# A bidirectional RWKV-7 scan on TensorE: the second direction's data move to the other head's partitions, and the fillers get a new order

## The reference, cut to what matters

```python
def step(S, inp):
    r_t, w_t, k_t, v_t, a_t, b_t = inp
    sa = einsum('zdhij,zdhj->zdhi', S, a_t)
    S = S * w_t + sa[..., :, None] * b_t[..., None, :] + v_t[..., :, None] * k_t[..., None, :]
    y = einsum('zdhij,zdhj->zdhi', S, r_t)
    return S, y
```

## Time and profile before

| | us |
|---|---|
| median of 3 runs | 2592.85 (2590.28 to 2593.1) |
| profiled execution: span from first to last instruction | 2592.7 |
| main loop of the scan, t = 0 to 39, in that execution | 593.71 |
| TensorE busy in the span | 2466.9 |
| VectorE, ScalarE, GpSimd busy in the span | 1183.0, 720.9, 806.8 |

### The profile page before, as it was taken

The page is one execution under the profiler, slowest core; times in us unless marked ns, Lnnn a source line. Parts: engine busy times, 40 slices in busy tenths (PEclk is TensorE's granted clock), DMA queues, the critical chain, the costliest instruction groups (busy, mean ns, idle before and its releaser), DMA issues. The chain is left out here.

```text
span 2592.7 us, 63094 instructions
## 1 busy us (share of the span) xinstructions
PE 2466.9 (95%) x27732; PEld 2043.2 (79%) x27732; DVE 1183.0 (46%) x2490; ACT 720.9 (28%) x1804; POOL 806.8 (31%) x623
## 2 busy tenths in 40 slices
PE   7999999999999699999999889999999999999997
PEld 6785568888888588778888767878888888888885
DVE  4105660000233466665766475554444444444446
ACT  5115661011111355645545432211110001110013
POOL 3322212222232233333333264023333224332234
PEclk9999999999999799999999989999999999999999
DMA  6110011111110100000000062211101010111014
GB/s 166 45 33 18 1 50 65 74 73 58 49 41 25 43 4 4 4 4 4 4 4 4 3 252 90 84 54 49 41 34 40 33 48 34 41 41 33 33 65 146
DMA packets 39085, 123.08 MB, mean 47 GB/s; under 512 B 11424, under 2 KB 11424, under 8 KB 37664
## 3 DMA queue, kind: packets, MB, share of 16 engines
q1 hardware_dynamic: 38816, 119.06, 13.5%
HBM read 96.24 MB, written 20.97 MB: 45 GB/s over the span
## 5 line engine op out<-in xcount | busy, mean ns | idle before, releaser
L2122 DVE TENSOR_TENSOR ff_f<-ff_f,ff_ps 128x512 f32<-128x512 f32 x300 | 205.3, 686 | 173.7 <-PE ff_ps L98 173.7
L2039 ACT ACTIVATE ff_rl<-ff_ps 128x512 f32<-128x512 f32 (+1 forms) x96 | 50.6, 527 | 754.9 <-PE ff_ps L98 754.9
L2141 DVE TENSOR_TENSOR ff_sq<-ff_rl 128x512 f32<-128x512 f32 (+1 forms) x96 | 125.5, 1308 | 271.9 <-ACT ff_rl L2039 271.7
L1058 DVE TENSOR_TENSOR sc_q<-sc_ps,sc_cs 128x128 f32<-128x128 f32 x400 | 98.4, 281 | 195.5 <-PE sc_ps L465 193.7
L1908 POOL TENSOR_TENSOR ff_wd0h<-ff_wdr,params 128x1024 fp32r<-128x1024 f32 x16 | 30.3, 1894 | 458.7 <-DMA ff_wdr<-in_w_down 458.7
L815 ACT ACTIVATE sc_xy<-sc_ps 128x256 f32<-128x256 f32 x320 | 116.5, 387 | 173.1 <-PE sc_ps L481 171.0
L481 PE MATMUL sc_ps<-sc_xy,sc_q 64*64 64x64 f32 x3200 | 150.7, 221 | 6.7 <-DVE sc_q L1058 6.0
L98 PE MATMUL ff_ps<-hh,ff_wu0h 128*128 128x512 f32 (+1 forms) x384 | 136.6, 356 | 4.4 <-issue 4.4
L98 PE MATMUL ff_ps<-hl,ff_wu0h 128*128 128x512 f32 (+1 forms) x384 | 136.3, 355 | 0.0
L98 PE MATMUL ff_ps<-hh,ff_wu0l 128*128 128x512 f32 (+1 forms) x384 | 136.3, 355 | 0.0
L98 PE MATMUL ff_ps<-hh,ff_wu1h 128*128 128x512 f32 (+1 forms) x384 | 136.0, 354 | 0.0
(11 more groups left out here) (323 smaller groups left out, 7007.2 us busy)
## 6 DMA issues: line engine op xcount, KB each, us to landing
ff_wur<-in_w_up SPq DMA_DIRECT2D x32, 512.0 KB, 3.5
ff_wdr<-in_w_down SPq DMA_DIRECT2D x32, 512.0 KB, 4.3
gwr<-in_w_in SPq DMA_DIRECT2D x31, 512.0 KB, 3.5
gm_dram<-gp_gm SPq DMA_DIRECT2D x8, 1280.0 KB, 4.4
ff_m<-gm_dram SPq DMA_DIRECT2D x16, 640.0 KB, 7.8
fr_x<-in_x SPq DMA_DIRECT2D x10, 512.0 KB, 5.1
ff_xs<-in_x SPq DMA_DIRECT2D x10, 512.0 KB, 4.5
x_dram<-ff_xo SPq DMA_DIRECT2D x10, 512.0 KB, 2.9
```

Source lines behind the costliest of these rows:

```text
L1058: nc.vector.tensor_tensor(Q1[g][:, :, :], q_out[g], joins[:, l, :].rearrange("p (u t) -> p u t", u=2), ALU.mult).then_inc(q_ready, 1)
L2039: nc.scalar.activation(rl[v % 2][:, 0:tn], ps[:, b, 0:tn], ACT.Relu).then_inc(relu, 1)
L2122: nc.vector.tensor_tensor(own, own, ps[:, 4 + v % 4, :], ALU.add).then_inc(added, 1)
L2141: nc.vector.tensor_tensor(sq[v % 2][:, 0:tn], rl[v % 2][:, 0:tn], rl[v % 2][:, 0:tn], ALU.mult).then_inc(squared, 1)
```

## The change

Direction 1's data that lie by token (the gram GM, the tokens TK with v now among them, P, U, the state S) move to the partitions of the other head (`on(rows, u)`), so `gram_and_tokens` (the two old functions in one), `outputs` and the others go straight for u = 0 and across for u = 1. Y changes sides from level to level (`y_side`); the flips and VT are gone, and v is turned each time. Arrays a and r of direction 1 and its edges are copied to the other half by two SBUF-to-SBUF transfers a step into SW (SyncE, semaphores `swapped`). The state is the sum of the new part and the old state, then multiplied by the edge, in two VectorE operations, and `keep` is gone. The gram is masked in one operation of 128x512, and the token copy waits for it. The fillers get another order on all three engines.

```diff
-        AR = [sb(f"sc_ar{n}", [P, 4, 2, BT]) for n in range(2)]
-        edge = [sb(f"sc_edge{n}", [P, GR, 2]) for n in range(2)]
+        AR = [sb(f"sc_ar{n}", [P, 2, ENDS + 4 * BT]) for n in range(2)]
+        SW = [sb(f"sc_sw{n}", [P, 2 * ENDS + 2 * BT]) for n in range(2)]
+        array = lambda par, n: AR[par][:, :, ENDS + n * BT:ENDS + (n + 1) * BT]
+        two = lambda par, rows, u, n, g: AR[par][rows, u, ENDS + n * BT:ENDS + (n + 2) * BT].rearrange(
+            "p (n t) -> p n t", n=2)[:, :, chunk(u, g)]
+        own_edge = lambda par: AR[par][:, 1, 0:ENDS]
+        edges = lambda par: SW[par][:, 0:2 * ENDS].rearrange("p (u g) -> p u g", u=2)
...
-        TK = [sb(f"sc_tk{g}", [P, 2, 2, C]) for g in range(GR)]
+        TK = [sb(f"sc_tk{g}", [P, 2, 3, C]) for g in range(GR)]
...
+        on = lambda rows, side: other[rows.start] if side else rows
...
+        def y_side(l, g, u):
+
+            if l == 0:
+                return u
+            if g % HALF == 0:
+                return 1 if l == LEVELS else 0
+            return l % 2
+
+        def q_cross(l, g, u):
+
+            return u ^ y_side(l, g, u)
+
+        def y_cross(l, g, u):
+
+            return y_side(l, g, u) ^ y_side(l + 1, g, u)
...
+            for q in range(STEPS):
+                sp.wait_ge(arr_ready, q + 1)
+                for rows in heads:
+                    sp.dma_start(SW[q % 2][on(rows, 1), ENDS:], AR[q % 2][rows, 1, 0:ENDS + 2 * BT]
+                                 ).then_inc(swapped[q % 2], 16)
...
+            def gram_and_tokens(q, g):
+                ct, i = divmod(q, NB)
                 n = q * GR + g
                 pe.wait_ge(arr_ready, q + 1)
                 if n:
                     pe.wait_ge(masked, n)
-                x = AR[q % 2]
-                for u in range(2):
-                    for m, lhs in enumerate((2, 3)):
+                    pe.wait_ge(tok_ready, n)
...
+                for m in range(2):
+                    for u in range(2):
                         for rows in heads:
+                            nc.tensor.matmul(gram_out[on(rows, u), u, m * 2 * C:(m + 1) * 2 * C],
+                                             array(q % 2, 2 + m)[rows, u, chunk(u, g)], two(q % 2, rows, u, 0, g),
+                                             start=True, stop=True)
+                for m, unit in enumerate((neg_eye, eye)):
+                    for u in range(2):
+                        for rows in heads:
+                            nc.tensor.matmul(tok_out[on(rows, u), u, m * C:(m + 1) * C],
+                                             array(q % 2, 2 + m)[rows, u, chunk(u, g)], unit[rows, :],
+                                             start=True, stop=True)
                 for u in range(2):
                     for rows in heads:
+                        last = nc.tensor.matmul(tok_out[on(rows, u), u, 2 * C:3 * C],
+                                                sT[rows, ct + 2 * CT, tokens(i, u, g)], eye[rows, :],
+                                                start=True, stop=True)
                 last.then_inc(tok_ps, 1)
...
+            def next_x(q, l, g):
+                for u in range(2):
+                    side = y_side(l, g, u)
+                    for rows in heads:
+                        last = nc.tensor.matmul(x_at(l, g, u)[on(rows, u), :], y_in(l, g, u)[on(rows, side), :],
+                                                Q1[g][on(rows, side), u, :], start=True, stop=True)
+                return last
+
+            def next_y(q, l, g):
+                for u in range(2):
+                    side, to = y_side(l, g, u), y_side(l + 1, g, u)
+                    for rows in heads:
+                        last = nc.tensor.matmul(y_at(l, g, u)[on(rows, to), :], Q1[g][on(rows, side), u, :],
+                                                y_in(l, g, u)[on(rows, side), :], start=True, stop=True)
+                return last
...
+                if l == LEVELS - 1:
+                    last = next_y(q, l, g)
+                elif g % HALF == 0:
+                    next_x(q, l, g)
+                    last = next_y(q, l, g)
+                else:
+                    next_y(q, l, g)
+                    last = next_x(q, l, g)
...
+                        a = SW[q % 2][:, 2 * ENDS:2 * ENDS + BT] if u else AR[q % 2][:, 0, ENDS:ENDS + BT]
...
+                pe.wait_ge(s_ready, n + 1)
...
-                if inner:
-                    solved(qs, sa)
-                if levels:
+                    pe.wait_ge(masked, q * GR + gb + 1)
                     pe.wait_ge(tok_ready, q * GR + gb + 1)
                 side(t, 0)
                 if ahead:
                     lora_products(q + 2)
+                if inner:
+                    solved(qs, sa)
                 if levels:
                     level_q(q, 1, ga)
                     level_q(q, 1, gb)
                 if inner:
                     state_out(qs, sa)
-                    outputs(qs, sa)
                 if levels:
                     level_xy(q, 1, ga)
                     level_xy(q, 1, gb)
+                side(t, 1)
                 if ahead:
                     pe.wait_ge(ta_ready, q + 3)
                 if more:
-                    gram_products(qa, sa)
-                if inner:
-                    state_in(qs, sb_)
+                    gram_and_tokens(qa, sa)
                 if levels:
                     level_q(q, 2, ga)
                     level_q(q, 2, gb)
-                side(t, 1)
-                if more:
-                    by_token(qa, sa)
                 if inner:
-                    solved(qs, sb_)
+                    outputs(qs, sa)
                 if levels:
                     level_xy(q, 2, ga)
                     level_xy(q, 2, gb)
                 if inner:
-                    state_out(qs, sb_)
-                if more:
-                    pe.wait_ge(masked, qa * GR + sa + 1)
-                side(t, 2)
-                if more:
-                    pe.wait_ge(tok_ready, qa * GR + sa + 1)
-                side(t, 5)
+                    state_in(qs, sb_)
                 if levels:
                     level_q(q, 3, ga)
                     level_q(q, 3, gb)
                 if inner:
-                    outputs(qs, sb_)
-                side(t, 3)
-                if more:
-                    gram_products(qa, sb_)
+                    solved(qs, sb_)
                 if levels:
                     level_xy(q, 3, ga)
                     level_xy(q, 3, gb)
+                if more:
+                    pe.wait_ge(masked, qa * GR + sa + 1)
+                    pe.wait_ge(tok_ready, qa * GR + sa + 1)
+                side(t, 2)
+                side(t, 5)
+                if inner:
+                    state_out(qs, sb_)
                 if levels:
                     level_q(q, 4, ga)
                     level_q(q, 4, gb)
+                side(t, 3)
                 side(t, 4)
                 if more:
-                    by_token(qa, sb_)
+                    gram_and_tokens(qa, sb_)
+                if inner:
+                    outputs(qs, sb_)
                 if levels:
                     level_xy(q, 4, ga)
                     level_xy(q, 4, gb)
-                if t + 1 < PAIRS:
-                    flip(qa, sa)
-                    flip(qa, sb_)
...
+                act.wait_ge(masked, n + 1)
+                nc.scalar.activation(TK[g][:, :, :, :].rearrange("p u n t -> p u (n t)"), tok_out,
...
-                if inner:
-                    u_copy(qs, sa)
-                    keep(qs, sa)
                 if ahead:
                     lora_tanh(q + 2, 0)
                     lora_tanh(q + 2, 1)
+                if inner:
+                    u_copy(qs, sa)
                 if squares_y and t % 2:
                     y_square(ct - 1, 1)
                 if levels:
...
                     level_copy(q, 1, gb)
                 if late:
                     decays(q + 1, 0)
-                if inner:
-                    p_copy(qs, sb_)
-                    keep(qs, sb_)
+                if levels:
+                    level_copy(q, 2, ga)
+                    level_copy(q, 2, gb)
                 if more:
                     token_copy(qa, sa)
                 if inner:
-                    u_copy(qs, sb_)
-                if levels:
-                    level_copy(q, 2, ga)
-                    level_copy(q, 2, gb)
+                    p_copy(qs, sb_)
                 if late:
                     decays(q + 1, 1)
+                if inner:
+                    u_copy(qs, sb_)
                 if squares_y and t % 2 == 0:
                     y_square(ct - 1, 0)
+                if levels:
+                    level_copy(q, 3, ga)
+                    level_copy(q, 3, gb)
                 if squares_y and t % 2:
                     y_std(ct - 1, GRAM_BANK)
                 if t % 2 and i == 0 and ct + 1 < CT:
                     k_norm(ct + 1, TOK_BANK)
```

(44 more changed lines are left out.)

254 lines of the change are left out of this document (114 added, 140 removed).

## The result

The changed kernel takes 2610.6 us (median of four runs, 2609.1 to 2615.1), the kernel before 2591.6 on the same chip: a ratio of 1.007, 95% interval 1.0058 to 1.0082, slower by 0.7%. The forecast was 2585.

A forecast was written before the change was run, and what follows sets the result against it. TensorE, busy 95% of the span, was taken as the bound. Half step terms, side work, reciprocals and GpSimd waits summed to 585.5 us for the loop against 593.7, -8.2, giving 2585 us, own range 2570 to 2600.

The forecast's parts named there:

- TensorE's saving: Products on other array quarters, mainly gram, tokens, outputs and flips: 2.05 to 2.6 us less per half step, 82 to 105 over 40.
- The idle time before the second chunk's level_q: At the start of a half step TensorE waits for collect, mask and the chain to the transpose: some 1.4 us idle.
- Odd half steps with LoRA products: 18 of 20 odd half steps: 14.5 us each, slower than before, with 2.24 for u_copy and 0.33 for half.
- Even ones without side products: Six even half steps: 11.95 us each, plus 0.7 for VectorE operations waiting on GpSimd.
- The transfers: Two SBUF transfers per step: hidden, first read a half step after the gram; up to 5 us a step if not covered.
- Rival 3: Gram, tokens and outputs do not run four quarters wide: 1.6 us a half step back on the path, 2650; chance 0.05.
- rival 1: Queues hurt less, half of the 1.4 idle and of 2.24 in nine odd half steps goes: 2547; chance 0.13.
- the sum: All loop terms added: 585.5 us against 593.7, so -8.2 and a kernel of 2585.
- rival 4: New idle stretches bring ten more TensorE stretches at 1.2 GHz: +12 us, 2597; chance 0.12.
- the even half steps with side products: 14 even half steps: 11.95 us plus 2.4 for side products, and 0.2 for GpSimd.
- The 2.24 us of u_copy behind the tanh: Odd half steps: state_out waits for u_copy behind four tanh and starts at 11.97 instead of 9.73; bounds 1.5 and 2.6.
- Rival 2: GpSimd blocks the new state multiply and AI in every even half step, 40 us instead of 7: 2618; chance 0.20.

The follow-up runs named there:

- experiment 8: The changed kernel with each gram product made twice into the same columns: 2637.9 us, ratio 1.0179.
- experiment 3: The changed kernel with three extra unused products between the first products of the first and second chunk of each half step: 2603.5 us, ratio 1.0043.
- experiment 10: VectorE's add, multiply, transpose of the first group and half of the LoRA step put behind level 3's joins: changed kernel 2619.1 us, the improved version 2583.2.
- Experiment 1: The changed kernel with u_copy put back ahead of the tanh, and solved ahead of the side and LoRA products: 2593.0 us, ratio 0.9997.
- experiment 11: State update's decay multiply moved from VectorE to ScalarE as two scaled copies: changed kernel 2608.1 us, the improved version 2572.5.
- the improved version: The changed kernel with u_copy ahead of the tanh, the last collect behind the next group's start, and three extra products in the gap: 2579.8 us, ratio 0.9945.
- experiment 7: The changed kernel with gram and token products issued direction by direction, neighbours two quarters at a time: 2614.3 us, ratio 1.0079.

## Why the prediction was wrong, by its own steps

**Right.** TensorE's saving: 2.05 to 2.6 us a half step forecast, 2.0 less busy time measured (just under the lower bound, with 27 us more of the loop at half clock), and in experiment 8 added work costs most of its price. The idle time before the second chunk's level_q: 1.4 us forecast, 58.7/39 = 1.5 measured. Odd half steps with LoRA products: 14.5 plus reciprocal, by_head and GpSimd (together 0.8 to 0.9) is 15.3 to 15.4, and those at full clock take 15.4. Even ones without side products: 11.95 + 0.7 = 12.65, against 12.58 for t = 2 and 13.35 for t = 6. The transfers never appear as a releaser. Rival 3 is out (a block of 20 products for grams and tokens takes 0.79 us, as reckoned for four quarters), and rival 1 is too: the wait for the transpose is as long as said.

**The step that failed is the sum: it left out rival 4 and took the even half steps with side products and the end of the loop too short.** The loop is 20.7 us longer than the sum (606.2 against 585.5). About 10 of it is half clock, as worked out above; the forecast had this as rival 4 with +12 and a chance of 0.12, on the ground that "the new gaps are followed by denser products". The runs speak against that ground: each half step now opens with a gap of 1.5 us in the mean, and five of the seven stretches at 1.2 GHz start in or right behind such a gap. With useless products in it, half clock in the loop falls to 3.4 us and the kernel is 7 us faster (experiment 3); with VectorE's work merely shifted, half clock doubles and the kernel is 8 us slower (experiment 10). Another 5 us is the even half steps with side products, 15.1 in the mean of the twelve at full clock where the terms give 14.7 (11.95, 2.4 for sides, 0.2 GpSimd, and the reciprocals). The last three, t = 37 to 39, take 43.1 us together where the terms give 36.6 (twice 11.95 and 12.65): 6.5 more, for which no run gives the cause. On the other side t = 0 took 11.7 where the terms give 14.65, and the place between start_group and join(3) has 12 reciprocals in the loop, not 16 (48 of them by the profile, four to a half step), so 1.8 us of the sum had nothing behind it. That leaves some 4 us unassigned. Outside the loop are another 2 us, where the forecast had 0.5: 2.8 more behind it, 0.8 less ahead of it. The step from sum to sign needed 8 us of margin, and these terms are larger than that.

**One term was right in sum and wrong in its parts.** The 2.24 us of u_copy behind the tanh was booked on the new order. Undone, it gives 1.0 us a half step (17.6 us over 18), and in the old kernel the order costs 1.6. The 2.24 was counted from an even half step, which has no LoRA products; these (1.1 us of TensorE) come in either order and were inside the 2.24. Experiment 1 agrees: with the order put back, odd half steps with LoRA products but no by_head still take 14.1 us at full clock against 13.1 for t = 2, 4 and 6. So 2.24 - 1.1 is about what the order costs. Still, this one decision is as large as the whole slowdown: without it the changed kernel is level with the one before.

**Rival 2** was right about the blocked multiply (594 against 288 ns; 18 of the 66 take over 1 us, which the forecast had named as a sign of being wrong, and 20 us of waiting in all where it had put 12.4 on GpSimd) and wrong about its place: experiment 11 gives 2.5 us alone, within the error, and 7 on the improved version.

So, where the 79.5 us of saved TensorE work went: TensorE's idle time in the loop grew by 92.0 us, the 79.5 and the 12.5 by which the loop is longer. Of it, 58.7 us are the wait for a transpose whose chain starts at the end of a half step, and 25.7 the wait for u_copy. The cost of half clock, about 10, is not in this account: it shows mostly as busy time, not as waiting. The first was part of the forecast and is only partly shown by runs: taking 0.45 us out of VectorE's path gave 10 us. Why the chain starts so late stays partly open: the mask waits for the outputs, and the outputs for the state's multiply, since they now lie in two banks of PSUM, one of them that of the state product. That last wait is small as it stands: 5.8 us of TensorE's idle time in the loop. Another placing was not tried, nor was the new layout with the old order of fillers.

## What to carry to other kernels

Denser products only help if what hands them their input gets shorter too: add up TensorE's idle time by releaser before and after, not its busy time. When a change opens a regular gap, count the clock as part of its price from the start; here it took about as much as the whole forecast gain, and cheap products in the gap made it visible in one run. Before putting anything ahead of a copy on an in-order engine, ask who waits for the copy: moving one 0.29 us copy behind four tanh, and the products that feed it behind the LoRA products, cost 18 us.

## What the runs showed of the hardware

- Products for free quarters start ahead of earlier ones in the queue, so the order of issue costs less than it seems. Given two quarters at a time, a block still came out at 0.92 us against 0.79 (the expectation's estimate was 1.35). Its timeline in experiment 7 shows ten records of L493 starting ahead of the first of L497, though only eight stand ahead of it in the program:

```profile
1183.03 0.41 PE L493 MATMUL sc_ps<-sc_cs,sc_ar 64*64 64x64 f32 x10
1183.26 0.22 PE L497 MATMUL sc_ps<-sc_cs,sT 64*64 64x64 f32 x2
```

- The granted clock moves with small shifts of work on other engines: 3.4, 17.1, 37.5 and 71.7 us at half clock in loops that differ by a few operations.
- Three extra 128x128 by 256-column products in each of 40 half steps add 47 us of busy time in 555 us and take 7 us off the kernel.
- A VectorE operation with both inputs in SBUF took 1089 ns in the mean beside a running GpSimd operation and 292 without one; with one input in PSUM it took 280 to 293 ns either way.
